# Spreading the reciprocal norms with rounded pairs in place of plain fp32

## The reference

```
u = rmsnorm(x) ; q,k,v of two attentions = u @ w_in
h = x + concat(window attention, differential attention) @ w_out
z = rmsnorm(h) @ w_up ; h = h + relu(z)^2 @ w_down
h = h + sigmoid(rmsnorm(h) @ w_gate) * (p @ w_ple)
y = rmsnorm(h)
rmsnorm(x) = x * rsqrt(mean(x*x) + 1e-6) * gain
```

## Time and profile before

| what | before |
|---|---|
| median of three runs | 1217.61 us (1216.28 to 1219.97) |
| the profiled execution | 1215.57 us |
| its span, first to last instruction | 1213.7 us |
| TensorE busy | 1191.8 us, 98% |
| VectorE / ScalarE / GpSimd busy | 710.8 / 518.6 / 600.2 us |
| granted TensorE clock, mean | 0.996 |

### The profile page before, as it was taken

One profiled execution on the slowest core, in us unless ns is written; L12 is line 12 of the kernel. 1 busy time (PEld: TensorE's weight loads), 2 busy tenths in 40 slices (PEclk: granted clock), 3 DMA queues, 4 the chain that ended last, 5 costly groups with the idle time before them and its releaser, 6 DMA issues.

```text
span 1213.7 us, 14773 instructions
## 1 busy us (share of the span) xinstructions
PE 1191.8 (98%) x5825; PEld 964.1 (79%) x5825; DVE 710.8 (59%) x927; ACT 518.6 (43%) x858; POOL 600.2 (49%) x284
## 2 busy tenths in 40 slices
PE   6999999999999999999999999999999999999997
PEld 5787787877677788888888888888888888888886
DVE  5245556566767457783937829478294692544233
ACT  6435445455655554423424243243342433442223
POOL 3323222232425567655565556655466555565542
PEclk8999999999999999999999999999999999999999
DMA  6811011123612333425234252342523423121203
GB/s 220 282 36 35 18 36 30 40 53 70 191 36 73 101 125 150 177 70 199 95 122 139 70 183 100 134 139 70 176 102 127 151 70 139 52 78 55 58 1 139
DMA packets 104123, 125.75 MB, mean 104 GB/s; under 512 B 21801, under 2 KB 87382, under 8 KB 98678
## 3 DMA queue, kind: packets, MB, share of 16 engines
q1 hardware_dynamic: 103814, 124.18, 31.2%
q10 hardware_dynamic: 240, 0.62, 0.1%
HBM read 111.14 MB, written 16.01 MB: 105 GB/s over the span
## 4 chain that ended last, share of the span: by engine, by line
PE 94%; DVE 3%; ACT 2%; DMA 1%; SPq 0%; issue 0%; DVEq 0%; ACTq 0%
PE ps L1811 51%; PE ps L1495 23%; PE ps L1471 8%; PE ps L1606 3%; PE ps L1629 3%; PE ps L1617 1%; PE ps L1693 1%; PE ps L1679 1%; PE ps L1666 1%; DMA x_raw<-in_x 1%; ACT e_a L1099 1%; PE ps L1538 1%; PE ps L1554 0%; PE ps L1509 0%; PE ps L1799 0%
## 5 line engine op out<-in xcount | busy, mean ns | idle before, releaser
L883 POOL TENSOR_TENSOR w_lo<-w_raw,w_hi 128x1024 fp32r<-128x1024 f32 x57 | 137.9, 2419 | 148.0 <-ACT w_hi L1008 146.9
L1811 PE MATMUL ps<-block_lo,w_hi 128*128 128x512 f32 x472 | 181.1, 389 | 0.0
L1495 PE MATMUL ps<-u_hi,w_hi 128*128 128x512 f32 x416 | 176.3, 424 | 3.8 <-DVE o_bt L2090 1.7
L752 POOL TENSOR_TENSOR w_lo<-w_raw,w_hi 128x1024 fp32r<-128x1024 f32 x38 | 96.1, 2529 | 163.9 <-ACT w_hi L1023 163.9
L1811 PE MATMUL ps<-up_hi,w_hi 128*128 128x512 f32 x448 | 174.9, 390 | 0.0
L1811 PE MATMUL ps<-up_hi,w_lo 128*128 128x512 f32 x448 | 174.3, 389 | 0.0
L1811 PE MATMUL ps<-up_lo,w_hi 128*128 128x512 f32 x448 | 174.3, 389 | 0.0
L1811 PE MATMUL ps<-block_hi,w_hi 128*128 128x512 f32 x440 | 172.0, 391 | 0.0
L1811 PE MATMUL ps<-block_hi,w_lo 128*128 128x512 f32 x440 | 171.3, 389 | 0.0
L1495 PE MATMUL ps<-u_hi,w_lo 128*128 128x512 f32 x416 | 163.4, 393 | 0.0
L1495 PE MATMUL ps<-u_lo,w_hi 128*128 128x512 f32 x416 | 162.8, 391 | 0.0
(11 more groups left out here) (224 smaller groups left out, 2091.8 us busy)
## 6 DMA issues: line engine op xcount, KB each, us to landing
up_lo<-lo_save SPq DMA_DIRECT2D x36, 1024.0 KB, 5.5
w_raw<-in_w_in SPq DMA_DIRECT2D x48, 256.0 KB
w_raw<-in_w_down SPq DMA_DIRECT2D x18, 512.0 KB
w_raw<-in_w_up SPq DMA_DIRECT2D x16, 512.0 KB
raw_x<-in_w_up SPq DMA_DIRECT2D x15, 512.0 KB
raw_x<-in_w_down SPq DMA_DIRECT2D x14, 512.0 KB
x_raw<-in_x SPq DMA_DIRECT2D x8, 512.0 KB, 7.3
h_save<-x_t SPq DMA_DIRECT2D x1, 4096.0 KB, 12.8
```

Of the source, the lines that this page charges most:

```text
L752: nc.gpsimd.tensor_tensor(w_lo[:, s * D:(s + 1) * D], w_raw[:, s * D:(s + 1) * D], w_hi[:, s * D:(s + 1) * D].bitcast(F32), ALU.subtract). ...
L883: nc.gpsimd.tensor_tensor(w_lo[:, s * D:(s + 1) * D], raw, w_hi[:, s * D:(s + 1) * D].bitcast(F32), ALU.subtract).then_inc(lo_done, 1)
L1495: mm = nc.tensor.matmul(bank(bank_), w, xx[:, x0], start=(first and n == 0), stop=(last and n == 2))
L1811: mm = nc.tensor.matmul(o, w, xx, start=(first and m == 0), stop=(last and m == 2), skip_group_check=onto)
```

## The change

`spread` no longer multiplies plain fp32. VectorE rounds `rs8` to fp32r (`rs8_hi`, a 128x8 copy), waits for that, and subtracts to get the remainder `rs8_lo` (128x8). It then makes two diagonal arrays: `diag_hi` where `diag` was, and `diag_lo` at one of two other places. TensorE multiplies ones in fp32r with both, and adds them up in PSUM: four matmuls for two. `spread` waits for both arrays. In the gate block `spread(3, 6)` moves from ahead of k=3 to ahead of k=4, and `turn_second` from k=5 to k=6. The array of ones is declared fp32r and read as fp32 by the sums of squares; these stay as they were.

```diff
--- before.py
+++ after.py
@@ -232,7 +232,8 @@
         w_hi = at("w_hi", [P, 2 * D], F32R, a_ring + 8 * KB_)
         w_lo = at("w_lo", [P, 2 * D], F32R, a_ring + 16 * KB_)
         rstd = at("rstd", [P, T], F32, a_rstd)
-        diag = at("diag", [P, TT * P], F32, a_rstd)
+        diag_hi = at("diag_hi", [P, TT * P], F32R, a_rstd)
+        diag_lo = [at("diag_lo0", [P, TT * P], F32R, a_z + 64 * KB_), at("diag_lo1", [P, TT * P], F32R, a_u + 60 * KB_)]
         acc_mlp = at("acc_mlp", [P, T], F32, a_rstd)
         acc = at("acc", [P, T], F32, a_acc)
         lam_in = at("lam_in", [P, 4 * HD], F32, a_acc)
@@ -244,7 +245,8 @@
         def small(name, n, parts=P):
             return at(name, [parts, n], F32, area((4 * n + 31) // 32 * 32))
 
-        ident, ones = small("ident", P), small("ones", P)
+        ident = small("ident", P)
+        ones_r = at("ones_r", [P, P], F32R, area(4 * P))
         g_col = small("g_col", 33)
         relb = small("relb", 12, NBUCKET)
         sink, nsink = small("sink", 8), small("nsink", 8)
@@ -258,6 +260,8 @@
         ssq, mean = small("ssq", 8), small("mean", 8)
         ssq_b = small("ssq_b", 16)
         rs8 = small("rs8", 8)
+        rs8_hi = at("rs8_hi", [P, TT], F32R, area(32))
+        rs8_lo = small("rs8_lo", 8)
         mean_b = small("mean_b", 8)
         rs_b = small("rs_b", 8)
         mhalf, gb = small("mhalf", 8), small("gb", 1)
@@ -338,6 +342,7 @@
         stat = sem("stat")
         mean_ok, pow_ok = sem("mean_ok"), sem("pow_ok")
         diag_ok, rs_ps, rstd_ok = sem("diag_ok"), sem("rs_ps"), sem("rstd_ok")
+        rs_split = sem("rs_split")
         h_saved = sem("h_saved")
         first_ok = sem("first_ok")
 
@@ -756,7 +761,7 @@
             pool.wait_ge(gpool, 1)
             nc.gpsimd.affine_select(out=ident[:, :], in_=ident[:, :], compare_op=ALU.not_equal, fill=1.0, base=0,
                                     pattern=[[-1, P]], channel_multiplier=1).then_inc(const_ok, 1)
-            nc.gpsimd.memset(ones[:, :], 1.0).then_inc(const_ok, 1)
+            nc.gpsimd.memset(ones_r[:, :].bitcast(F32), 1.0).then_inc(const_ok, 1)
             nc.gpsimd.memset(mhalf[:, :], -0.5).then_inc(const_ok, 1)
             for t in range(0, TT, 2):
 
@@ -1504,10 +1509,11 @@
 
             def spread(n, bank_):
 
-                pe.wait_ge(diag_ok, n)
+                pe.wait_ge(diag_ok, 2 * n)
                 for i in range(2):
-                    mm = nc.tensor.matmul(bank(bank_ + i), ones[:, :], diag[:, i * HALF:(i + 1) * HALF],
-                                          start=True, stop=True)
+                    for m, d in enumerate((diag_hi, diag_lo[n % 2 == 0])):
+                        mm = nc.tensor.matmul(bank(bank_ + i), ones_r[:, :], d[:, i * HALF:(i + 1) * HALF],
+                                              start=(m == 0), stop=(m == 1))
                 mm.then_inc(rs_ps, 1)
 
             def bank_for(name, half):
@@ -1796,7 +1802,7 @@
                 pe.wait_ge(sq_ok, (DT + 1) * n + DT - missing)
                 for t in range(TT):
                     o = bank_ * 512 + t
-                    mm = nc.tensor.matmul(ps[:, o:o + 1], squares[:, t * P:(t + 1) * P], ones[:, 0:1], start=True,
+                    mm = nc.tensor.matmul(ps[:, o:o + 1], squares[:, t * P:(t + 1) * P], ones_r[:, 0:1].bitcast(F32), start=True,
                                           stop=True)
                 mm.then_inc(stat, 1)
 
@@ -1959,7 +1965,7 @@
             pe.wait_ge(ple_in, 16)
             turn_ple(0)
             pe.wait_ge(mean_ok, 3)
-            gate_block(1, hooks={3: lambda: spread(3, 6), 5: turn_second})
+            gate_block(1, hooks={4: lambda: spread(3, 6), 6: turn_second})
             pe.wait_ge(ple_lo_ok, 2)
             ple(0, 0, free=False)
             ple(1, 1, free=False)
@@ -1992,7 +1998,7 @@
                 pe.wait_ge(sq_last, r + 1)
                 for t in range(4 * r, 4 * r + 4):
                     mm = nc.tensor.matmul(ps[:, 6 * 512 + TT + t:6 * 512 + TT + t + 1], sqt[:, t * P:(t + 1) * P],
-                                          ones[:, 0:1], start=True, stop=True)
+                                          ones_r[:, 0:1].bitcast(F32), start=True, stop=True)
                 mm.then_inc(stat, 1)
 
             pe.wait_ge(part_ok, 1)
@@ -2062,9 +2068,17 @@
             def diagonals(n):
 
                 dve.wait_ge(pow_ok, n)
-                nc.vector.tensor_tensor(diag[:, :].rearrange("p (t q) -> p t q", q=P),
+                nc.vector.tensor_copy(rs8_hi[:, :], rs8[:, :]).then_inc(rs_split, 1)
+                dve.wait_ge(rs_split, 2 * n - 1)
+                nc.vector.tensor_tensor(rs8_lo[:, :], rs8[:, :], rs8_hi[:, :].bitcast(F32), ALU.subtract).then_inc(rs_split, 1)
+                nc.vector.tensor_tensor(diag_hi[:, :].rearrange("p (t q) -> p t q", q=P),
                                         ident[:, :].unsqueeze(1).to_broadcast([P, TT, P]),
-                                        rs8[:, :].unsqueeze(2).to_broadcast([P, TT, P]), ALU.mult).then_inc(diag_ok, 1)
+                                        rs8_hi[:, :].bitcast(F32).unsqueeze(2).to_broadcast([P, TT, P]),
+                                        ALU.mult).then_inc(diag_ok, 1)
+                dve.wait_ge(rs_split, 2 * n)
+                nc.vector.tensor_tensor(diag_lo[n % 2 == 0][:, :].rearrange("p (t q) -> p t q", q=P),
+                                        ident[:, :].unsqueeze(1).to_broadcast([P, TT, P]),
+                                        rs8_lo[:, :].unsqueeze(2).to_broadcast([P, TT, P]), ALU.mult).then_inc(diag_ok, 1)
 
             dve.wait_ge(x_ss, TT)
             mean_square(1, ssq[:, :])
```

## The result

The changed kernel is slower: median 1221.07 us, against 1217.01 us of the kernel before on the same chips, a ratio of 1.0026 with a 95% interval of 1.0016 to 1.0037. That is 3.2 us (1.9 to 4.5). One of the changed kernel's eight executions took 5590 us and is left out of the ratio but not of its median, so the text goes by the ratio's 3.2 us and not by the 4.1 us between the medians. Forecast was a gain of 0.4 us, with a range that ended at 1219.9.

A forecast was written before the change was run, and what follows sets the result against it. TensorE, busy for 98% of the span, was taken as the bound. Norms 1, 2 and 3 summed as -0.81 + 1.1 - 0.7 = -0.4 us, to 1217.2 us against the median of 1217.61, range 1214.7 to 1219.9.

The forecast's parts named there:

- The gain of 0.81 us each: At each of three spreadings, four fp32r matmuls take 0.91 us for 1.72; 2.4 us for three.
- Norm 1 covered: At norm 1 the arrays are ready at 41.4, 1.4 us before TensorE needs them; -0.81 us.
- Norm 2: One GpSimd operation gets in between copy and subtraction; TensorE waits 1.9 us, net +1.1 us.
- rival 3: At norm 2 GpSimd gets in twice, spreading 4.3 us late; sum +2.0 us, 1219.6; chance 0.13.
- the wait of VectorE for its own result: Between the small copy and the subtraction, each time, VectorE waits some 0.03 us.
- Back to back: At norm 2 the two diagonal arrays follow the subtraction without a gap, ending at 481.3 and 482.5.
- `w_lo` hidden: At norm 2 the fifth block's `w_lo` ends at 484.8, before TensorE asks for it at 486.1.
- Norm 3: At norm 3 -0.81 + 0.1 = -0.7 us, bounds -0.8 and -0.3; a possible TensorE wait of 0.4 us.
- The moved hooks: At norm 3, spreading six matmuls later pays for itself: at the old place TensorE would wait 1.1 us or more.
- The hidden alternative: At norm 2 VectorE goes first, GpSimd's subtraction runs afterwards, and TensorE waits 0.8 us for `w_lo`.
- rival 2: At norm 2 VectorE keeps its turn and GpSimd pays; norm 2 nothing, sum -1.5 us, 1216.1; chance 0.15.

The follow-up runs named there:

- hi_first: The changed kernel with the 128x8 rounding on ScalarE and VectorE's first diagonal array ahead of the small subtraction; single execution, norm 2 at 613.51 us (+5.5).
- stall5: The kernel before, plain fp32, with five unused VectorE reductions ahead of norm 2's diagonal array; single execution, norm 2 grew by 5.35 us.
- act_hi: The changed kernel with the 128x8 rounding on ScalarE instead of VectorE; ratio 0.9997 (0.9986 to 1.0009) to the kernel before.
- reduce_hi: The changed kernel with the 128x8 copy made by a VectorE maximum over rows of one element; ratio 1.0022 to the kernel before, +2.7 us.
- n13_hold: The changed kernel with plain fp32 at norm 2 and GpSimd waiting for both arrays at norm 3; ratio 0.9991 to the kernel before, -1.1 us.
- hold2: The changed kernel with GpSimd waiting for both diagonal arrays at norms 2 and 3; ratio 1.0011 (1.0003 to 1.0020) to the kernel before.
- swap: The changed kernel with GpSimd's fifth-block `w_lo` ahead of its `s_sum` subtraction; ratio 1.0012 (1.0003 to 1.0021) to the kernel before.

## Why the prediction was wrong

**The gain of 0.81 us each** was right: four matmuls in 0.90 us for 1.72. The stretch of norm 1 agrees with it as far as its scatter allows (-0.76 in the kernel after; -0.19 to -0.86 over all profiles with the pair there).

**Norm 1 covered** was right: the second array was ready at 43.20 and TensorE came at 44.87, 1.7 us later.

**Norm 2 is the step that failed**, at the sentence that has the copy pass while GpSimd gets in behind it ("VectorE's copy follows, which reads one array"). I had taken only operations that read two arrays to be exclusive with GpSimd. The copy is one too (2.40 us; a reduction in its place 0.14). So GpSimd's first operation was spent on the copy, and its second came ahead of the subtraction. TensorE lost 3.95 us where I had 1.9. The size was that of rival 3 (4.3 us), the place another: rival 3 had the second operation come in behind the subtraction. I gave it 0.13. Whether the wait of VectorE for its own result, priced at 0.03 us, had a part in it isn't shown: in hi_first the second operation got in without one.

The prediction's own rows held the answer, and it misread them. It has GpSimd begin L840 in the gap between VectorE's two small operations, but 323.71 lies ahead of the first one's end at 323.77. And that first one was held up as well: it took 0.38 us, where the same line takes 0.16 when undisturbed, and ended as L752 did (323.74). So two small operations, one after the other, had each waited for a GpSimd operation of its own. Norm 2 did the same with two long ones.

**The clock was not in the sum.** The text costs a wait of TensorE at its length. After 3.95 us of idle time it ran at half clock, which cost 2.6 us more; stall5 shows the same kind of loss, 1.4 us, without the change. The range ended 2.3 us above the time before, and 3.2 were lost: without the 2.6 us of the clock the time would have stayed inside it, as it would with a wait of 1.9 us in place of 3.95. With the clock's part, rival 3 would have read +4.6 us and not +2.0.

**Back to back.** The forecast let VectorE keep its turn from `diag_hi` to `diag_lo`, on the ground of one pair of rows. In eight profiles with GpSimd's `s_sum` waiting and VectorE's next operation right behind L2317, VectorE went first in two. Between the two arrays at norm 2 it went first in act_hi and not in reduce_hi. In the kernel after it didn't matter, as GpSimd had nothing ready by then. What decides such a meeting stays open; the operation's size doesn't (3.42 us for a big one in hi_first and n13_hold).

**`w_lo` hidden** held. **Norm 3** was -0.55 for -0.7: the wait of 0.4 us that the text named as its bound is there, because of two collisions. The moved hooks were judged rightly (1.39 us). **The hidden alternative** in rival 2, GpSimd put last, was underpriced: hold2 shows 0.9 us at `w_lo`, as computed, and another 2.4 us at the down weights.

## What to carry to other kernels

An operation of 0.15 us on the path costs what it may have to wait for. In a stretch where GpSimd works on arrays in SBUF, count one whole GpSimd operation for each VectorE copy and for each VectorE operation that reads two arrays there; the reduction was free of it here (0.14 us). Price TensorE's idle time with the clock behind it: waits of 3.8 to 4.0 us cost more than their length here, waits of 1.7, 2.8 and 3.3 us didn't bring the clock down. Before moving the other engine's work out of the way, follow what its result and its buffer release: here that had less than 1.6 us to spare.

## What the runs showed of the hardware that I had not expected

A 128x8 copy within SBUF took 2.37 to 2.40 us with a GpSimd subtraction running and 0.16 to 0.17 without; the same rounding as a reduction took 0.14 with GpSimd running. The meeting of the same two instructions, `diag` and GpSimd's `s_sum`, came out as 1.22 and 3.90 us in one execution and as 3.42 and 2.77 in another. And a wait of 3.9 us cost 5.35 in a kernel in which 2.8 us cost 2.64; behind a wait of 3.3 us (swap) the clock was still 1.00.
